# A fifth block-product group per pair in the down projection, and one weight sum per group by an adding transfer

## The reference, cut to what matters

```python
def pool_mixer(...):   ...  return (mixed * scale * jax.nn.silu(g)) @ w_out    # [256, 4096] @ [4096, 2048]
def mla_mixer(...):    ...  return (o * jax.nn.silu(g)) @ w_out                # [256, 2048] @ [2048, 2048]
def conv_ffn(h, w_up, conv_w, conv_b, w_down):
    ...
    return (jax.nn.silu(g) * val) @ w_down                                     # [256, 5504] @ [5504, 2048]
def second_block(...):
    ...
    x = x + conv_ffn(rms_norm_2(x, norm_ffn[l]), w_up[l], conv_w[l], conv_b[l], w_down[l])
    return rms_norm_2(x, norm_final)       # x / sqrt(mean(x*x) + eps) * norm_final
```

## Time and profile before

| what | value |
|---|---|
| runs | 2435.7, 2435.97, 2436.27 us |
| profiled execution, first to last instruction | 2434.2 us |
| TensorE (PE) busy | 2423.9 us, 100% |
| VectorE (DVE) busy | 1720.3 us, 71% |
| ScalarE (ACT) busy | 1373.7 us, 56% |
| GpSimd (POOL) busy | 64.7 us, 3% |
| TensorE's granted clock, mean | 0.999 |
| DMA, mean | 186 GB/s |

### The profile page before, as it was taken

The page is one execution under the profiler, slowest core; times in us unless marked ns, Lnnn a source line. Parts: engine busy times, 40 slices in busy tenths (PEclk is TensorE's granted clock), DMA queues, the critical chain, the costliest instruction groups (busy, mean ns, idle before and its releaser), DMA issues.

```text
span 2434.2 us, 33996 instructions
## 1 busy us (share of the span) xinstructions
PE 2423.9 (100%) x12679; PEld 2084.6 (86%) x12679; DVE 1720.3 (71%) x2083; ACT 1373.7 (56%) x1823; POOL 64.7 (3%) x79
## 2 busy tenths in 40 slices
PE   9999999999999999999999999999999999999998
PEld 8888888888889999888888888888988888888887
DVE  7675757899765656796756667665767657679887
ACT  6444444556656666565755556565644545455555
POOL 0000000001100000010000000000000000000001
PEclk9999999999999999999999999999999999999999
DMA  8666666565555554565585554454565565656654
GB/s 314 199 189 185 188 189 183 188 218 199 180 175 181 179 158 147 211 212 189 165 235 163 161 171 151 164 178 154 172 191 180 189 190 180 191 169 205 220 184 145
DMA packets 234595, 453.03 MB, mean 186 GB/s; under 512 B 14929, under 2 KB 60417, under 8 KB 233324
## 3 DMA queue, kind: packets, MB, share of 16 engines
q1 hardware_dynamic: 230960, 435.94, 55.9%
q0 software_dynamic: 3120, 14.90, 1.7%
q10 hardware_dynamic: 396, 0.59, 0.2%
HBM read 448.68 MB, written 2.69 MB: 185 GB/s over the span
## 4 chain that ended last, share of the span: by engine, by line
PE 99%; DVE 1%; ACT 0%; issue 0%; ACTq 0%; DVEq 0%
PE ps L813 25%; PE ps L815 13%; PE ps L779 12%; PE ps L781 12%; PE ps L780 12%; PE ps L963 6%; PE ps L964 6%; PE ps L965 6%; PE ps L737 1%; PE ps L844 1%; PE ps L846 1%; PE ps L845 1%; PE ps L1443 1%; PE ps L1214 0%; PE ps L1202 0%; PE ps L1401 0%
## 5 line engine op out<-in xcount | busy, mean ns | idle before, releaser
L2443 DVE TENSOR_TENSOR w_lo<-raw,w_hi 128x1024 fp32r<-128x1024 f32 x689 | 842.1, 1228 | 466.7 <-ACT w_hi L1613 446.8
L1613 ACT ACTIVATE w_hi<-raw 128x1024 fp32r<-128x1024 f32 x689 | 726.8, 1060 | 650.9 <-PE ps L815 357.7
L813 PE MATMUL ps<-x_hi_lo,w_hi 128*128 128x512 f32 x2336 | 821.0, 394 | 0.0
L815 PE MATMUL ps<-x_hi_lo,w_lo 128*128 128x256 f32 x2336 | 660.7, 283 | 0.0
L813 PEld LDWEIGHTS ps<-x_hi_lo,w_hi 128*128 128x128 f32 x2336 | 438.8, 188 | 101.2
L779 PE MATMUL ps<-w_hi,x_hi_lo 128*128 128x512 f32 (+3 forms) x1184 | 461.9, 390 | 0.0
L781 PE MATMUL ps<-w_hi,x_hi_lo 128*128 128x512 f32 (+3 forms) x1184 | 453.7, 383 | 0.0
L780 PE MATMUL ps<-w_lo,x_hi_lo 128*128 128x512 f32 (+3 forms) x1184 | 452.7, 382 | 0.0
L815 PEld LDWEIGHTS ps<-x_hi_lo,w_lo 128*128 128x128 f32 x2336 | 439.3, 188 | 0.0
L1790 ACT ACTIVATE w_hi<-raw 128x1024 fp32r<-128x1024 f32 (+1 forms) x201 | 209.4, 1051 | 169.8 <-PE ps L965 152.2
L2451 DVE TENSOR_TENSOR w_lo<-raw,w_hi 128x1024 fp32r<-128x1024 f32 (+1 forms) x201 | 243.2, 1228 | 35.4 <-ACT w_hi L1790 35.1
(11 more groups left out here) (469 smaller groups left out, 2711.9 us busy)
## 6 DMA issues: line engine op xcount, KB each, us to landing
raw<-in_w_up SPq DMA_DIRECT2D x160, 512.0 KB, 3.9
raw<-in_pool_w_in SPq DMA_DIRECT2D x126, 512.0 KB, 3.8
raw<-in_w_in SPq DMA_DIRECT2D x96, 480.0 KB, 3.8
raw<-in_w_down SPq DMA_DIRECT2D x84, 512.0 KB, 5.1
raw<-in_pool_w_out SPq DMA_DIRECT2D x64, 512.0 KB, 4.8
raw<-in_ple_w_gate SPq DMA_DIRECT2D x64, 512.0 KB, 4.3
raw<-in_mla_w_in SPq DMA_DIRECT2D x56, 448.0 KB, 3.5
raw<-in_pool_w_group SPq DMA_DIRECT2D x32, 512.0 KB, 4.1
```

The lines of the kernel that those rows point to most:

```text
L813: pe.matmul(bank, w_hi[:, slot, cols], xs[:, k].rearrange("p s n -> p (s n)"), start=k == 0, stop=False, skip_group_check=True)
L815: last = pe.matmul(bank[:, 0:T], w_lo[:, slot, cols], xs[:, k, 0, :], start=False, stop=k == nkt - 1, skip_group_check=True)
L1613: act.activation(w_hi[:, t.slot(), :], raw[:, slot, :], ACT.Copy).then_inc(S("w_hi"), 1)
L2443: dve.tensor_tensor(w_lo[:, t.slot(), :], raw[:, u % RAW, :], w_hi[:, t.slot(), :].bitcast(F32), ALU.subtract)\
```

## The change

1. **Down gets a fifth group in each pair.** `DOWN_QUADS` has 20 as a first tile beside 24, 28, 32 and 36; a pair has 24 plain units and 5 groups, with three plain units between groups in most places and two ahead of the last. The activation sums grow from four to five groups (from 1024 to 1280 elements a row each); they lie lower in the memory arena. The pieces of the activations' splits and their steps are set anew.
2. **One weight sum per group is made by a transfer.** GpSimd issues a DMA from one slot of `raw` to another that adds (`accum_op=ALU.add`), once both are loaded and the add before is done. VectorE makes three sums. Signs of the activation sums and of the readouts are adapted to it.
3. **The order inside a group** is B11, B22, T1, B21, T3, T2, T4, where it was B11, B22, T1, T3, B21, T2, T4, and B12 is loaded ahead of B11. Each bank's last product is found by a table (`closing`).
4. **The final norm weights come in four pieces** of 512 columns: piece 1 at the end of up, the others after the last group of down, since the activation sums now lie where they go. The squares in the second pair are moved to other steps.
5. The mask of the attention shares the semaphore of the identity matrix.

```diff
-DOWN_QUADS = [24, 28, 32, 36]
+DOWN_QUADS = [20, 24, 28, 32, 36]
-DOWN = [D0[:10] + DQ[0] + D1[:4] + DQ[1] + D1[4:8] + DQ[2] + D1[8:12] + DQ[3] + D1[12:] + D0[10:],
-        D2[:4] + DQ[0] + D2[4:8] + DQ[1] + D2[8:12] + DQ[2] + D3[:4] + DQ[3] + D2[12:] + D3[4:]]
-DOWN_Y_STEPS = {6: 3, 7: 4, 11: 5, 13: 6, 17: 7, 22: 8}
+DOWN = [D0[:9] + DQ[:1] + D1[:3] + DQ[1:2] + D1[3:6] + DQ[2:3] + D1[6:9] + DQ[3:4] + D1[9:11] + DQ[4:] + D1[11:] + D0[9:],
+        D2[:4] + DQ[:1] + D2[4:7] + DQ[1:2] + D2[7:9] + D3[:1] + DQ[2:3] + D3[1:4] + DQ[3:4] + D3[4:6] + DQ[4:] + D2[9:] + D3[6:]]
+DOWN_Y_STEPS = {6: 3, 7: 4, 8: 5, 10: 6, 12: 7, 15: 8, 19: 9}
...
-                loads += [(j1, 2 * p), (j1, 2 * p + 1), (j2, 2 * p + 1), (j2, 2 * p)]
-                released += [products + 3, products + 3, products + 5, products + 6]
+                loads += [(j1, 2 * p + 1), (j1, 2 * p), (j2, 2 * p + 1), (j2, 2 * p)]
+                released += [at[part] for part in LAST_USE]
...
+                b12, b11, b22, b21 = (raw[:, (u + n) % RAW, :] for n in range(4))
+                product_lo(raw[:, (u + SLOT_OF[kind]) % RAW, :])
+                if kind == "B22":
+                    dve.wait_ge(S("w_added"), 16 * (t.n.get("quad", 0) + 1))
+                    dve.tensor_tensor(b22, b22, b12, ALU.add).then_inc(S("w_sums"), 1)
+                elif kind == "T1":
+                    dve.wait_ge(S("w_sums"), 3 * t.n.get("quad", 0) + 1)
+                    dve.tensor_tensor(b11, b22, b11, ALU.subtract).then_inc(S("w_sums"), 1)
+                elif kind == "T3":
+                    dve.tensor_tensor(b21, b21, b22, ALU.add).then_inc(S("w_sums"), 1)
...
-            if n in (23, 26):
-                square_out((26 - n) // 3)
-            if n == 30:
+            if n in (21, 23):
+                square_out((23 - n) // 2)
+            if n == 28:
                 square_out(2)
...
+        def weight_sums(units):
+            for u in units:
+                b12, b11 = (raw[:, (u + n) % RAW, :] for n in range(2))
+                for v in (u, u + 1):
+                    pool.wait_ge(S(f"raw_full{v % RAW}"), 16 * (v // RAW + 1))
+                if t.n["quad"]:
+                    pool.wait_ge(S("w_added"), 16 * t.n["quad"])
+                pool.dma_start(b12, b11, accum_op=ALU.add).then_inc(S("w_added"), 16)
+                t.add("quad")
...
             if n == 0:
+                weight_sums(pool_out.weight_sums[:1])
                 products(pool, "pool", 8)
             load(pgain, a["post_norm"][n:n + 1, :].broadcast_to([128, D]), "post_gain_in")
+            if n == 0:
+                weight_sums(pool_out.weight_sums[1:])
...
+                if n == 1 and c == 0:
+                    weight_sums(mla_out.weight_sums)
...
         products(pool, "up")
-        load(fgain, a["norm_final_2"].unsqueeze(0).broadcast_to([128, D]), "final_gain_in")
+        final_gain(1)
+        weight_sums(down.weight_sums)
+        pool.wait_ge(S("w_used"), RING + down.quads_end[1])
         pool.wait_ge(S("final_gain_in"), 16)
+        for c in (0, 2, 3):
+            final_gain(c)
```

More of the change, by code:

```diff
@@ L70, with plain, quads_at @@
 TOTAL_UNITS = UNITS_END["down"]
+PARTS = ("B11", "B22", "T1", "B21", "T3", "T2", "T4")
+SLOT_OF = {"B12": 0, "T1": 0, "B11": 1, "T3": 1, "B22": 2, "T2": 2, "B21": 3, "T4": 3}
+LAST_USE = ("T1", "T3", "T2", "T4")
+def plain(c, kts):
+    return [("plain", c, kts)]
+def quads_at(first_tiles):
+    return [[(part, n, k) for part in PARTS] for n, k in enumerate(first_tiles)]
 POOL_QUADS = [20, 24, 28]
-P0, P1, P2, P3 = ([("plain", c, (k, k + 1)) for k in range(0, 20, 2)] for c in range(NCH))
-PQ = [[("quad", n, k)] for n, k in enumerate(POOL_QUADS)]
@@ L86 @@
-DOWN_Y_STEPS = {6: 3, 7: 4, 11: 5, 13: 6, 17: 7, 22: 8}
-DOWN_Y = [(0, 8), (8, 16), (16, 24), (24, 28), "sums", (28, 32), (32, 36), (36, 40), (40, 43)]
-MLA_OUT_QUADS = [8, 12]
[L91 to L98, removed]
+DQ = quads_at(DOWN_QUADS)
@@ L99, in quad_tables, with paired_tables @@
+MQ = quads_at(MLA_OUT_QUADS)
+MLA_OUT = [[], M2[:3] + MQ[:1] + M3[:2] + MQ[1:] + M2[3:] + M3[2:]]
+def paired_tables(first_unit, pairs, before):
+    loads, released, quads_end, plain_end, steps, units = [], [], [], {}, [], []
     last_quad = 0
     products = first_unit + before
-    for p, steps in enumerate(pairs):
-        for kind, c, kts in steps:
+    for p, pair in enumerate(pairs):
+        steps.append([])
+        for entry in pair:
+            unit = first_unit + len(loads)
+            steps[-1].append([(kind, c, kts, unit) for kind, c, kts in entry])
+            at = {kind: products + n for n, (kind, _, _) in enumerate(entry)}
+            products += len(entry)
+            kind, c, kts = entry[0]
@@ L1071, in pair @@
                     pe.wait_ge(S(f"mm_free{s}"), t.at(f"set{s}", 1))
-                steps = x.steps[p][:-len(ending)] if p == 1 and ending else x.steps[p]
-                for kind, c, kts in steps:
-                    if (kind == "quad" or c == 2 * p + 1) and begins("all sets"):
+                steps = parts[:-len(ending)] if p == 1 and ending else parts
+                for i, (kind, c, kts, _) in enumerate(steps):
+                    if (kind != "plain" or c == 2 * p + 1) and begins("all sets"):
                         for s in range(2):
@@ L3058, in mixed_sums @@
                 stepped()
-                step(dve.tensor_tensor(msums[:, a11], msums[:, a22], msums[:, a11], ALU.subtract))
+                step(dve.tensor_tensor(msums[:, a11], msums[:, a22], msums[:, a11], ALU.add))
                 stepped()
@@ L3670, in _ @@
             for tt in range(2):
-                last = pool.tensor_tensor(h[:, tt, cols], h[:, tt, cols], fgain[:, cols], ALU.mult)
+                last = pool.tensor_tensor(h[:, tt, cols], h[:, tt, cols], fgain[c], ALU.mult)
             last.then_inc(S("final_gained"), 1)
```

260 lines of the change are left out of this document (131 added, 129 removed).

## The result

The changed kernel takes 2439.62 us (median of 20 runs, 2438.19 to 2440.75); the kernel before, run beside it, 2436.12 us (20 runs, 2435.58 to 2436.8). The ratio is 1.0014, 95% interval 1.0008 to 1.002. The sign is settled, and the size is under the 0.2% that I had called no change. The forecast was 2435.3, a gain of 0.7 us, in a range that ended at 2438.4: the result lies 4.3 us above the one and 1.2 us above the other.

A forecast was written before the change was run, and what follows sets the result against it. TensorE, busy 100% of the span, was taken as the bound, with VectorE having least to spare. 2435.97 - 2.8 + 1.1 + 1.2 = 2435.5, less 0.2 in the pool stage: 2435.3 us; range 2432.8 to 2438.4.

The forecast's parts named there:

- Term 1: Down: one more group in each of two pairs removes 12 matmuls of 0.2315 us from TensorE, -2.78 us.
- Term 2: Start of down: VectorE's subtraction for T2 in the first group makes TensorE late once, +1.1 us (bounds 0 to 2).
- Term 3: Pool, MLA and down: 18 adding transfers of 512 KB within SBUF take 7.7 us each and cost 0.
- One of its signs: Adding transfers: no idle time of ScalarE or VectorE that ends with a DMA on the raw tiles.
- Term 4: End of the kernel: later read-out, squares and POOL's last product delay the final norm chain, +1.2 us (0 to 2.2).
- The pool stage: Out products of the pool layer: two short gaps before T2 go with a quicker VectorE, -0.2 us, an estimate.
- (a): First group and end: VectorE is in time and POOL's last product done by 2422.4; 2433.2 us, chance 0.26.
- (b): Ten groups in down and pool: the adding transfer is late, from about 10 us; 2437 to 2454, chance 0.11.
- (c): MLA layer: adds come after the memory loads and hold T1, up to 3 us; 2438, chance 0.04.

The follow-up runs named there:

- e4: Changed kernel with the first pair's first group of down one plain unit later, as before the change; 2438.04 us.
- e1: Changed kernel with down's four groups per pair and their places as before, all norm weights loaded at the end of up; 2436.04 us.
- e2: Changed kernel without GpSimd's six multiplications by the final norm weights; 2435.22 us.
- e3: Changed kernel with the second pair's groups earlier, eleven units' worth of plain products behind the last group instead of eight; 2435.18 us.
- e8: Changed kernel without GpSimd's first two products with the final norm weights, the third kept; 2435.35 us.

## Why the prediction was wrong, point by point

- **Term 1** (12 matmuls, -2.8): right. In the versions without late starts it comes out in the time, less what is left at the pair change.
- **Term 2** (first group, +1.1): right in place, cause and size: 1.2 us in two waits for VectorE's subtractions, gone when the group is moved (e4). VectorE began the group at 2220.8, where I had counted 2221.0, and ended T2's subtraction at 2231.2, as counted. I had it as one gap; the other, ahead of it at 2227.77, is the wait for the subtraction of B21, the fourth block product, for which I had counted no need time.
- **Term 3** (adds, 7.7 us, cost 0): right, 7.0 us and no cost to TensorE. One of its signs did not hold: ScalarE and VectorE each waited once for a transfer, in the MLA layer, though TensorE's starts stayed 0.23 us apart. That nothing would come of the lighter VectorE in the other stages was right too (e1).
- **Term 4** (the end, +1.2) is the step that failed. It followed only the chain through the norm: read-out, squares, GpSimd's product, VectorE's reduction. The same series of VectorE holds the subtractions for TensorE's last plain products, and I worked out no need time for these: TensorE's waits at the end stood at nothing and measured 2.3 us. The term also took the 14.4 us of read-out and subtractions over from the trace before, with its two stretched subtractions, though the products would now fall on other operations. In the changed kernel they stretch them by 4.3 us instead of 2.1, to 16.7 us. The tail grew by 1.9 where I had taken 1.2, within the 0 to 2.2 that I had allowed; what lies outside the range is the 2.3. Without the products, or with the read-out earlier, both go (e2, e3, e8).
- **Not in the forecast**: 0.4 us at the pair change. With fewer subtractions between the fifth group and the end of the pair, half of its read-out stands in one piece ahead of the next pair's first subtraction.
- **The pool stage** (-0.2, an estimate): TensorE's starts there are late by 0.3 us together in before and by 0.2 now, so 0.1 of it came.
- **The rivals**: (a), that the covers hold, was wrong in both places; it is what the moved tables give (2433.7 against its 2433.2). (b) and (c), adds so late that TensorE waits, did not occur. The mechanism that did, VectorE late for TensorE at the end, was none of my rivals, and so the range was too short at the top.

The sum by measured terms: -2.8 + 1.2 + 0.4 + 2.3 + 1.9 = +3.0, against +3.5 between the medians, whose interval reaches from 1.9 to 4.9. By single traces the remaining 0.5 can't be assigned.

## What to carry to other kernels

Where an engine is the one with the least to spare, take a series of its operations from a trace only together with what ran beside it: when it moves by some us, another operation meets the neighbour, and a stretch of 1 us can become one of 3. For such a series ask for every reader when it needs each result, not only for the chain to the end. And when a change adds work for a gain of a few microseconds, move the dense places (first group, read-out) before judging it: the same five groups cost 3.5 us in one table and gained 2.5 in another.

## What the hardware showed

**VectorE and GpSimd shut each other out.** Where a VectorE operation with both inputs in SBUF met GpSimd's product, one of the two stood until the other's instruction was done. The subtraction ended 1.09 us behind the product in the changed kernel (4.11 us long), and 1.08 in before (2400.18 + 2.23 against 2398.78 + 2.55). Operations with an input in PSUM kept their 0.68 us. In e3 it was GpSimd that waited, 4.39 us for 2.55, with VectorE at 1.21. And within the two instructions of one product both can lose, as beside the second product of before:

```profile
2405.67 3.68 POOL L3671 TENSOR_TENSOR h<-h,final_gain 128x512 f32<-128x512 f32 x2 [4.34 <-ACTq L2358]
```

```profile
2405.88 2.32 DVE L2451 TENSOR_TENSOR w_lo<-raw,w_hi 128x1024 fp32r<-128x1024 f32 x1
```

Which operations meet, the Trainium skill says on its page "SBUF — State Buffer", section "Who interferes with whom": a VectorE instruction with two SBUF inputs contends with a GpSimd instruction that reads SBUF, one with at most one SBUF input, outside the two-port modes, does not. The rows agree. Which of the two waits they don't let me foresee: in the changed kernel the subtraction starts 0.45 us ahead of GpSimd's product and waits, in e3 it starts 0.30 us ahead (2405.35 and 2405.65) and GpSimd waits.

**An adding transfer within SBUF** of 512 KB took 6.4 to 8.3 us (medians of the ten traces that have it; in down alone 5.6 to 9.7), and its issue occupied GpSimd 0.85 us where a plain load took 0.54.
